# Two-layer block on one core: the barriers between attention, routing and experts become waits, semaphores are cleared on the way, and the first gate split moves ahead

## The reference, cut to what matters

```python
def diff_attention(q, k, v, lam, subln_g, lam_init):      # 4 heads of 2 x 64, 8 query blocks of 128
    ...
        s = jnp.einsum("bqhcd,bkhcd->bhcqk", qi, k) * scale
        p = jax.nn.softmax(jnp.where(mask, s, -jnp.inf), axis=-1)
        a = p[:, :, 0] - lam * p[:, :, 1]
        return jnp.einsum("bhqk,bkhe->bqhe", a, v)

def hierarchical_moe(h, w_rg, b_rg, w_re, b_re, w_g, w_u, w_d):
    ...                                                   # group, then two of its eight experts
    order = jnp.argsort(e_flat, stable=True)              # rows put in blocks of 128 by expert
    ...
    def expert_block(args):
        xb = hf[toks]
        hid = jax.nn.silu(jnp.matmul(xb, w_g[e])) * jnp.matmul(xb, w_u[e])
        return jnp.matmul(hid, w_d[e]) * wb[:, None]
```

## Time and profile before

| | |
|---|---|
| three timed runs | 3044.0, 3046.55, 3046.78 us; median 3046.55 us |
| the profiled execution | 3043.43 us, its span 3041.6 us |
| mean granted clock of TensorE | 0.961 of full |
| busy, share of the span | PE 92%, PEld 75%, DVE 63%, ACT 47%, POOL 16% |

### The profile page before, as it was taken

How to read it: one execution, slowest core, us unless ns; L and a number is a source line. 1 busy time by engine, 2 the same in 40 slices (tenths; PEclk the granted TensorE clock), 3 DMA queues, 4 the chain that set the end, 5 groups by cost and what they waited for, 6 DMA issues and landing times. The chain is left out here.

```text
span 3041.6 us, 36124 instructions
## 1 busy us (share of the span) xinstructions
PE 2792.5 (92%) x13292; PEld 2281.5 (75%) x13302; DVE 1901.3 (63%) x2142; ACT 1440.0 (47%) x2105; POOL 482.1 (16%) x375
## 2 busy tenths in 40 slices
PE   6998999999989989999989987899899599999996
PEld 5787977888867666887878866778678488888874
DVE  3776745444345554435544876799563599888885
ACT  2544435323336655333333445533422277777773
POOL 0001400000006664000000000000000134434331
PEclk9999999999989999999999998999999699999998
DMA  3110011213466663121211100111212499999994
GB/s 93 42 49 15 1 57 42 101 46 104 159 187 132 139 131 77 49 104 42 91 56 51 49 15 1 29 46 46 89 53 116 172 364 384 369 366 368 363 356 150
DMA packets 159435, 387.95 MB, mean 128 GB/s; under 512 B 72769, under 2 KB 72897, under 8 KB 134720
## 3 DMA queue, kind: packets, MB, share of 16 engines
q1 hardware_dynamic: 150080, 369.27, 36.3%
q0 software_dynamic: 9216, 16.81, 2.2%
HBM read 347.93 MB, written 54.85 MB: 132 GB/s over the span
## 5 line engine op out<-in xcount | busy, mean ns | idle before, releaser
L2957 DVE TENSOR_TENSOR ex_w<-ex_raw,ex_w 128x2048 fp32r<-128x2048 f32 x190 | 430.8, 2289 | 77.5 <-ACT ex_w L2892 75.8
L2892 ACT ACTIVATE ex_w<-ex_raw 128x2048 fp32r<-128x2048 f32 x190 | 361.8, 1916 | 143.0 <-DMA ex_raw<-in_w_up_e 62.4
L2808 PE MATMUL ps<-ex_w,ex_xT 128*128 128x512 f32 x1536 | 368.3, 396 | 15.5 <-DVE ex_xT L2972 15.4
L2808 PEld LDWEIGHTS ps<-ex_w,ex_xT 128*128 128x128 f32 x1536 | 287.0, 190 | 82.0 <-issue 13.7
L945 DVE TENSOR_TENSOR bs_t<-arena,bs_t 128x1024 fp32r<-128x1024 f32 x88 | 107.7, 1224 | 270.0 <-ACT bs_t L898 269.9
L898 ACT ACTIVATE bs_t<-arena 128x1024 fp32r<-128x1024 f32 x88 | 93.3, 1061 | 294.6 <-PE ps L841 280.8
L741 DVE SCALAR_TENSOR_TENSOR arena<-arena,small 128x1023 f32<-128x1023 f32 (+9 forms) x168 | 213.5, 1271 | 3.6
L1276 POOL TENSOR_TENSOR fa_pl<-fa_p,fa_ph 128x512 fp32r<-128x512 f32 x192 | 191.9, 1015 | 103.5 <-ACT fa_ph L1397 100.8
L2808 PE MATMUL ps<-ex_w,ex_hT 128*128 128x512 f32 x768 | 182.9, 394 | 1.3 <-issue 1.1
L839 PE MATMUL ps<-bs_t,bs_w 128*128 128x512 f32 x448 | 175.3, 391 | 7.9 <-DVE bs_w L936 4.3
L840 PE MATMUL ps<-bs_t,bs_w 128*128 128x512 f32 x448 | 174.4, 389 | 0.0
(11 more groups left out here) (415 smaller groups left out, 6589.6 us busy)
## 6 DMA issues: line engine op xcount, KB each, us to landing
ex_raw<-in_w_gate_e SPq DMA_DIRECT2D x64, 1024.0 KB, 13.7
ex_raw<-in_w_up_e SPq DMA_DIRECT2D x64, 1024.0 KB, 13.1
ex_raw<-in_w_down_e SPq DMA_DIRECT2D x64, 1024.0 KB, 14.1
arena<-in_w_in SPq DMA_DIRECT2D x108, 512.0 KB, 3.5
arena<-in_x SPq DMA_DIRECT2D x4, 2048.0 KB, 11.1
arena<-in_w_out SPq DMA_DIRECT2D x16, 512.0 KB, 6.6
arena<-in_w_branch_ssm SPq DMA_DIRECT2D x8, 512.0 KB, 3.6
att_qh<-bs_split SPq DMA_DIRECT2D x2, 2048.0 KB, 8.8
```

What stands on the lines that cost most here:

```text
L2808: mm = nc.tensor.matmul(out, l, r, start=(k == 0 and n == 0), stop=(k == kc - 1 and n == 2))
L2892: nc.scalar.activation(half_of(part[m][0], h), raw[m][:, h * W // 2: (h + 1) * W // 2], ACT.Identity).then_inc(high[m], 1)
L2957: V.tensor_tensor(half_of(part[m][1], h), raw[m][:, h * W // 2: (h + 1) * W // 2], half_of(as_f32(part[m][0]), h), ALU.subtract)\
```

## The change

One block now reaches from the first layer's dense phase "bs" to the experts. The barriers and clears at the end of "q2" and of the routing go. In their place GpSimd clears the semaphores of finished phases while later ones run (`retire`), in two batches, and raises a semaphore `retired`, on which engines wait before they use semaphores of the next batch. The phases get the explicit waits that the barrier stood for. The second barrier at the end of `stage` (line 155) goes everywhere, so also after "xbc". And `used` of the experts is raised by PE in the routing, once the experts are chosen, so that ACT's first gate high parts can run there. The semaphores of the convolution norm, the gates and the routing are now cleared at the very end.

```diff
@@ Chip.stage
             with self.nc.Block() as block:
                 yield ctx, block
-        self.nc.all_engine_barrier()
+    def retire(self, block, sems, waits, retired):
+        @block.gpsimd
+        def _(pool):
+            for s, n in waits:
+                pool.wait_ge(s, n)
+            sems.close()
+            pool.sem_inc(retired, 1)
@@ phase_diff_attention, tensor
+            pe.wait_ge(retired, 1)
+            pe.wait_ge(normed, 2 * TT)
...
                 if x >= 8:
                     pe.wait_ge(low, x - 7)
+                else:
+                    pe.wait_ge(dense.by_act, 3 * TT + x + 1)
@@ phase_diff_attention, scalar
+            act.wait_ge(retired, 1)
+            act.wait_ge(dense.product, 5 * TT)
@@ phase_diff_attention, vector
+            dve.wait_ge(retired, 1)
+            dve.wait_ge(dense.tapped, taps)
+            dve.wait_ge(lam.params, 16 * 8)
@@ phase_out_route (vector, sync, scalar, tensor)
+            dve.wait_ge(retired, 1)
+            sp.wait_ge(retired, 1)
+            act.wait_ge(retired, 1)
+            pe.wait_ge(retired, 1)
...
             pe.wait_ge(step, at_step["chosen"])
+            for used in experts_may:
+                pe.sem_inc(used, 1)
@@ expert_programs, tensor
-        for m in range(3):
-            pe.sem_inc(used[m], 1)
+        if extra:
+            for m in range(3):
+                pe.sem_inc(used[m], 1)
@@ phase_experts
-    with ExitStack() as ctx:
-        main = expert_programs(...)
-        more = expert_programs(...)
-        block = ctx.enter_context(c.nc.Block())
+    with nullcontext(within) as (ctx, block):
@@ _build
-        with c.stage() as within:
+        with c.stage() as (alive, block):
+            first, second = (alive.enter_context(ExitStack()) for _ in range(2))
+            retired = [c.sem(alive, f"retired{n}") for n in range(2)]
+            ctx, within = first, (first, block)
...
+            c.retire(block, first, [(dense3.product, 2 * TT), (dense3.by_vec, TT), (dense3.w_low, 2 * KC + 1),
+                                    (out_normed.kept, 16 * TT)], retired[0])
-        with c.stage() as within:
-            differed = phase_diff_attention(c, q_tok, k_tok, lam, v2, o2, 4, 5, within)
+            differed = phase_diff_attention(c, q_tok, k_tok, lam, v2, o2, 4, 5, within, retired[0], dense3,
+                                            qk.normed, IN_Q2[-1])
+            ctx, within = alive, (alive, block)
...
+            c.retire(block, second, [(dense2.product, 2 * TT), (dense2.w_low, 2 * KC + 1)], retired[1])
+            main = expert_programs(c, ctx, "ex", xn, out[0], experts, raw, loaded, gathered)
+            more = expert_programs(c, ctx, "xe", xn, out[0], experts, expert_raw(c, True), main=main)
```

More of the change, by code:

```diff
@@ L9 @@
 from collections import namedtuple
-from contextlib import ExitStack, contextmanager
+from contextlib import ExitStack, contextmanager, nullcontext
 import concourse.bass as bass
@@ L989, in _ @@
                 end.on_vector(dve)
[L990 removed]
+    return Dense(product, by_act, by_vec, kept, w_low, NS, tapped)
 class GatedTurn:
@@ L1871, in on_scalar, with phase_diff_attention @@
             self.c.nc.scalar.wait_ge(self.stored, self.units)
-def phase_diff_attention(c, q_tok, k_tok, lam, v, o, q_region, k_region, within):
+def phase_diff_attention(c, q_tok, k_tok, lam, v, o, q_region, k_region, within, retired, dense, normed, taps):
     nc = c.nc
@@ L2256, in phase_out_route @@
                     w_expert, b_group, b_expert, tmp, region, x_first, gathered, prefetch,
-                    within, parts, dense):
+                    within, parts, dense, retired, experts_may):
     nc = c.nc
@@ L3022, in vector, with phase_experts @@
         run(dve, cycle)
-    return ExpertPrograms(sync, gpsimd, tensor, scalar, vector, half0, half1, stored)
-def phase_experts(c, x_dram, y_dram, experts, raw, loaded, gathered):
-    with ExitStack() as ctx:
-        main = expert_programs(c, ctx, "ex", x_dram, y_dram, experts, raw, loaded, gathered)
-        more = expert_programs(c, ctx, "xe", x_dram, y_dram, experts, expert_raw(c, True), main=main)
-        block = ctx.enter_context(c.nc.Block())
+    return ExpertPrograms(sync, gpsimd, tensor, scalar, vector, half0, half1, stored, used)
+def phase_experts(main, more, within):
+    with nullcontext(within) as (ctx, block):
         @block.sync
@@ L3060, in _, with _build @@
             more.vector(dve)
-def _build(nc, a, out, upto=99):
+def _build(nc, a, out):
     with ExitStack() as ctx:
@@ L3130, in _build @@
         shifts = nc.dram_tensor("att_shifts", (HEADS, TT, P), F32).ap()
-        if upto < 2:
-            return c
         phase_ssd(c, decays, c.at(1, 0, TT * TOK), R(4), R(3), 5)
-        if upto < 3:
-            return c
-        forget = ForgetSums(c, ctx, decays, R(1))
-        staged = [c.rounded(f"bs_split{n}", (3, 4)[n], 0, REGION // 2) for n in range(2)]
-        def heads_at(n, names):
-            return [att[m][n * BANK:(n + 1) * BANK, :].rearrange("(f p) s -> p f s", p=P) for m in names]
@@ L3175, in _build, with heads_at, fill_heads, first_heads @@
-        with c.stage() as within:
+        with c.stage() as (alive, block):
+            first, second = (alive.enter_context(ExitStack()) for _ in range(2))
+            retired = [c.sem(alive, f"retired{n}") for n in range(2)]
+            ctx, within = first, (first, block)
+            forget = ForgetSums(c, ctx, decays, R(1))
+            staged = [c.rounded(f"bs_split{n}", (3, 4)[n], 0, REGION // 2) for n in range(2)]
+            def heads_at(n, names):
+                return [att[m][n * BANK:(n + 1) * BANK, :].rearrange("(f p) s -> p f s", p=P) for m in names]
+            values_at = [[att[m].rearrange("(t p) d -> p t d", p=P)[:, :, n * BANK:(n + 1) * BANK]
+                          for m in ("vh", "vl")] for n in range(2)]
+            heads = Heads(c, ctx)
+            def fill_heads(pool, by_vec, kept):
+                pool.wait_ge(by_vec, 3 * TT)
+                heads.fill_a(pool)
+                pool.wait_ge(kept[9], 32)
+                heads.fill_b(pool)
+            def first_heads(sp, kept):
+                for j in (3, 6, 7, 8):
+                    sp.wait_ge(kept[j], 32)
+                for h in range(2):
+                    heads.load_a(sp, att, h)
+                sp.wait_ge(kept[9], 32)
+                heads.load_b(sp, att, 0)
+            gated_turn = GatedTurn(c, ctx, forget, R(3), R(4), R(1), c.at(1, 6 * SEQ, 2 * SEQ))
+            def beside_turn(n, tapped, by_act):
+                gated_turn.on_scalar(n)
+            def aside_turn(n, tapped, by_act, by_vec, moved):
+                forget.aside(n, tapped, by_act, by_vec, moved)
+                gated_turn.on_vector(n, by_act)
+            def split(n):
+                return (T(R(0)), wcol(w_in, (C_Q, C_K)[n // 2], n % 2), "split_T", staged[n % 2], None,
+                        heads_at(n % 2, (("qh", "ql"), ("kh", "kl"))[n // 2]),
+                        (float(HD) ** -0.5, 1.0)[n // 2])
@@ L3278, in _build @@
             assert IN_Q2[-1] + IN_GB2[-1] == CCH // P * CW, (IN_Q2[-1], IN_GB2[-1])
+            ctx, within = second, (second, block)
             lam = Lambdas(c, ctx)
@@ L3385, in _build @@
                             lambda sp, ms: load_expert(sp, raw, experts, 0, loaded, ms),
-                            within, parts2, dense2)
-        if upto < 10:
-            return c
-        phase_experts(c, xn, out[0], experts, raw, loaded, gathered)
+                            within, parts2, dense2, retired[1], main.used)
+            phase_experts(main, more, within)
         return c
```

42 lines of the change are left out of this document (3 added, 39 removed).

## The result

The changed kernel takes 3027.18 us, the median of four runs (3025.34, 3026.94, 3027.41, 3028.87), where the kernel before takes 3045.28 us, the median of four (the three runs of the table and one of 3040.06). The ratio is 0.994 with a 95% interval of 0.9923 to 0.9958, so faster by about 18 us (13 to 23). The profiled execution took 3027.41 us with a span of 3025.6 us and a mean granted clock of 0.962: 16.0 us less than the span before, at the same clock. Lines of code have moved by 10 to 27: line 2002 is now 2019, 2035 is 2055, 2045 is 2065, 2509 is 2531, 2808 is 2834, 2957 is 2984.

A forecast was written before the change was run, and what follows sets the result against it. PE was taken to bound the kernel almost everywhere, with gains where all engines stand still: 1.3 + 8.6 + 7.2 - 0.4 + 0.1 = 16.8 us, from 3046.55 to 3029.8 us, range 3023 to 3038.5.

The forecast's parts named there:

- After xbc, 1.3 us: After xbc, engines no longer wait for 14 clears; DVE starts at 285.6 against 286.90; bounds nothing and 2.03 us.
- what the start gains the stretch gains: Each stretch after the three changed joints only follows its start, so a gain at the start is kept in full.
- After q2, 8.6 us: Attention's start: ACT's first high part 8.3 us earlier, DVE's 16 low parts 0.3 us shorter; bounds 7.2 and 9.2.
- The cover of the clears: GpSimd's 109 clears (8.0 us) run beside q2 some 130 us before needed, 36 (2.6 us) in gb2; price zero.
- After the routing, 7.2 us: First expert product at 2414.5 instead of 2421.64, rows last to arrive, landing in 7.1 us; bounds 9.2 and 4.0.
- The early split buys nothing, and three raises cost 0.4 us: In the routing, ACT's early gate split shortens nothing on the chain; PE's raises of `used` before the ranking cost 0.4 us.
- The experts pass it on: In the experts, everything moves with the first product, so the 6.8 us net gain there is carried in full.
- not passed on: Rival: the experts' weight stream sets the end, so only 10.0 of 16.8 us are left; 3036.6 us, chance 0.08.
- the stream starts early and decides: Rival: expert 1's gate load goes out 13.1 us earlier and the end follows it; about 3023.8 us, chance 0.06.
- The gather is held longer: Rival: after the routing the rows land later, so that joint is worth 4.9 or 4.0 us; 3032 to 3034, chance 0.12.
- The clock: Rival: attention's mean clock falls to 0.74 and it grows by 23 us; 3053 us or more, slower chance 0.04.
- Clears late: Rival: the first batch is cleared late and attention waits, putting back up to 8.6 us; 3038.4 us, chance 0.02.

The follow-up runs named there:

- run with late clears: Changed kernel with the first batch of 109 clears allowed only after q2's last products and evictions: 3034.34 us, ratio 0.9972 to the kernel before.
- run with the late load: Changed kernel with SP's load of expert 1's gate weights waiting until expert 0's rows are split: 3025.74 us, ratio 0.9943 to the kernel before.

## Why the prediction was right

It had 3029.8 us and a range of 3023.0 to 3038.5 us; measured were 3027.18 us. Half of the 2.6 us between them is the kernel before, whose median is 3045.28 with its fourth run and was 3046.55 in the forecast; the gain was forecast as 16.8 us and is 18.1. Step by step:

- **After xbc, 1.3 us.** Measured 1.23 at the place, but in most profiles gone a hundred us later (100.8 us in the median of twelve profiles without the barrier, 100.5 and 100.6 in the two with it). Here the step "what the start gains the stretch gains" isn't borne out; the bound "nothing" that the forecast gave comes nearer.
- **After q2, 8.6 us.** Measured 8.35 (21.38 less 13.03). The 16 low parts take 10.62 us as worked out. The quarter of a microsecond is ACT's start: the forecast had it 0.14 us after the last V tile (1793.7 after 1793.56), and it came 0.42 us after it.
- **The cover of the clears.** 109, 36 and 153 were counted and are there. The forecast had 130 us of cover for the first batch, the trace shows 123. The run with late clears shows what the cover is worth: 9.8 us.
- **After the routing, 7.2 us.** Measured 10.0 (19.39 less 9.41). This is the term that was mis-sized, and in it one number: the landing of the rows, taken as 7.1 us, is 4.4, and these 2.7 us are the difference. The value taken came from gathers of the experts, which are issued into a stream that is already running. Here the gather is first, and a load that comes after it doesn't hold it (4.4 with and without). The lower bound of the landing, 5.1, was misread: the trace of before keeps one landing for the two issues of line 2509, at 2409.62, and 5.14 us is its distance from the second issue (2404.48). The forecast gave it to the first. A second gather with no load ahead of it takes 5.3 in the run with the late load too, where the first takes 4.4. The median of 7.1 in the row of line 2531 above is no agreement with the 7.1 of the forecast, but the mean of 4.4 and 9.8. The mechanism was right: the rows, not the weights, come last; ACT waits for PE and PE for the landing. DVE's first low part came 0.90 us behind the routing where the signs had 0.6.
- **The early split buys nothing, and three raises cost 0.4 us.** Both hold: 0.37 us by the idle time of DVE, and at most 0.1 to 0.2 us bought, which the scatter of this joint covers. The place of ACT's first high part was given as 2373.6, counting on 9.9 us gained until then; this profile had gained 6.2, since the attention and the state-space stretch ran longer. From before's 2383.55 less 6.2 it is 2377.3, the trace has 2377.0.
- **The end, 0.1 us.** 153 clears for 155, as counted.
- **The experts pass it on.** From first product to DVE's last instruction 592.5 before, 592.8, 592.0 and 590.0 after.

The sum by the measured places is 1.2 + 8.35 + 10.0 - 0.4 + 0.1 = 19.3 us, where the forecast had 16.8. Without the 1.2 after xbc it is 18.1, and the three series of the changed kernel give about 18 us; the stretches between the joints scatter by more than this difference, so the agreement proves little. The one profiled pair gives 16.0: the way to xbc is 0.9, the state-space stretch 3.1 and the attention 2.1 us longer in it than before, and the other stretches up to the routing's end are 2.7 us shorter. That the forecast of 16.8 comes so near to 16.0, and to within 1.3 us of 18.1, is thus partly luck: a term 2.7 us too small stood against slower stretches, and against 1.3 us after xbc that don't last.

The rivals: *not passed on* and *the stream starts early and decides* fell, the second by the late load and the first by the equal length of the experts. *The gather is held longer* did not happen, but it can: held by force it costs 8.2 us, more than the rival had (3). *The clock*: the attention's is 0.835 to 0.836 in three profiles of the changed kernel against 0.839 before (139.3 to 139.7 us against 137.6), and from 0.820 to 0.859 in the kernels of the experiments (135.9 to 140.8 us). So the forecast's own sign of being wrong, a lower clock in the attention, is there by 0.003 to 0.004; by the forecast's measure (0.01 is 1.9 us) this is 0.6 to 0.8 of the 1.7 to 2.1 us. One profile of before can't tell whether they belong to the change. *Clears late* appeared only when an edit brought it about.

On GpSimd's side of the gather the rows show this: an issue takes 1.02 to 1.22 us with DVE idle (the two of line 2509 in the kernel before), 1.90 when it starts 1.27 us into DVE's low parts, and 2.30 when it starts 1.20 us before the end of DVE's second half, ending 1.10 us after that half in both runs (2403.93 and 2402.83; 2395.57 and 2394.47). The Trainium skill (SBUF — State Buffer, section "SBUF: two separate sides") says that GpSimd can't write its descriptors while VectorE holds the port that they share, and gets in when VectorE's instruction ends. The trace agrees with that: in these three cases the price, 0.9 to 1.1 us, is near what was left of one DVE instruction of some 2.3 us (1.0 to 1.2). By the rule as the forecast put it the first gather would wait for one low part. It didn't: GpSimd started at 2396.75, DVE 0.26 us later, the issue took 1.23 us as if alone, and DVE's instruction wasn't slowed either (2.29 us). Nor does every instruction of DVE hold GpSimd: the issue at 2404.26 in the kernel after starts 0.02 us into DVE's low part of the rows, which reads one of its inputs from PSUM, and takes 1.02 us.

## What to carry to other kernels

A meeting of engines is cheap and what stands beside it is not. Here a meeting cost 0.7 us after q2 and 0.1 or nothing before the experts, and what GpSimd had to do at the same places, clears after q2, drain and clears after the routing, 8 and 10 us; look at what the barrier's last engine does before its overlap is redesigned, and move serial clears (66 to 73 ns each) beside a phase in which that engine is idle, those behind the last work too.

For a small transfer on the path that sets the start of a stage, ask what is issued before it, not what runs beside it: take its duration from the row of a gather that was first in its queues, make sure which of several issues a landing belongs to, and keep it ahead of the next large load.

Price a joint at its own place, between two instructions on either side of it; the end of the kernel carries the scatter of every stretch between. Then ask in several profiles whether the gain is still there one stretch later, before it is added to a sum: the 1.23 us after xbc were not.

## What the runs showed of the hardware

- A gather issued 1.0 us after the first issue of a weight's load (2 MB) landed in 9.0 us, one issued 2.6 us ahead of the same load in 4.4, and one with no load before it in 5.5. The issues of the 9.0 and the 5.5 both ran into DVE's low part and took 2.30 us, that of the 4.4 took 1.23.
- GpSimd's drain at the end of the block took 6.50 us in the kernel before, from 2403.3, between its two gather issues, to 2409.8, 0.2 us after the second gather's landing. After the last scatter of the kernel after, the same drain takes 5.30 us; those of ACT, PE and DVE there take 13 to 24 ns.
- One and the same kernel had a granted clock of 0.880 to 0.942 in the state-space stretch and 95.0 to 101.5 us for it. Nothing in the profiles says why. Of the twelve profiles without the second barrier after xbc ten have 0.875 to 0.887 there, the two with it 0.903 and 0.905.
- The loop over absent experts took GpSimd 6.7 us in one kernel and 9.4 in another whose code ahead of it differs by a few instructions.
